# A causal convolution's filter sums moved wholly onto TensorE, with their tile moves in ScalarE's queue

## The reference, cut to what matters

```
def conformer_conv(h, w_pw1, b_pw1, w_dw, b_dw, ln_g, ln_b, w_pw2, b_pw2):
    u = h @ w_pw1 + b_pw1
    a, gate = jnp.split(u, 2, axis=-1)
    u = a * jax.nn.sigmoid(gate)
    u = lax.conv_general_dilated(
        u, w_dw[:, None, :], window_strides=(1,), padding=[(CONV_WIDTH - 1, 0)],
        dimension_numbers=("NWC", "WIO", "NWC"), feature_group_count=CONV_CHANNELS) + b_dw
    u = jax.nn.silu(layernorm(u, ln_g, ln_b))
    return u @ w_pw2 + b_pw2
```

## Time and profile before

| | us |
|---|---|
| median of 3 runs | 1313.1 (1306.43 to 1316.91) |
| the profiled execution | 1311.96 |
| its span in the trace | 1310.6 |
| TensorE busy | 1210.4 (92%) |
| VectorE busy | 960.3 (73%) |
| ScalarE busy | 653.4 (50%) |

### The profile page before, as it was taken

One profiled execution on the slowest core, in us unless ns is written; L12 is line 12 of the kernel. 1 busy time (PEld: TensorE's weight loads), 2 busy tenths in 40 slices (PEclk: granted clock), 3 DMA queues, 4 the chain that ended last, 5 costly groups with the idle time before them and its releaser, 6 DMA issues.

```text
span 1310.6 us, 24770 instructions
## 1 busy us (share of the span) xinstructions
PE 1210.4 (92%) x9796; PEld 1152.6 (88%) x9796; DVE 960.3 (73%) x1853; ACT 653.4 (50%) x1142; POOL 108.7 (8%) x106
## 2 busy tenths in 40 slices
PE   4978899999998999999978788999989879999999
PEld 4957899999987999999967678999989767999999
DVE  5966598878776888878886658888875555766653
ACT  5326554445446544445555664544444765545431
POOL 2001100002000200004000112000011112100000
PEclk9999899999999999999998989999999989999999
DMA  7487688877853678787633325887865422555552
GB/s 275 142 210 92 225 301 261 252 265 265 271 179 123 196 262 263 236 276 249 219 110 103 103 91 177 272 255 252 275 230 184 133 89 83 191 179 186 184 193 65
DMA packets 81126, 259.36 MB, mean 198 GB/s; under 512 B 8904, under 2 KB 20424, under 8 KB 81012
## 3 DMA queue, kind: packets, MB, share of 16 engines
q1 hardware_dynamic: 81012, 257.79, 62.1%
HBM read 252.68 MB, written 5.08 MB: 197 GB/s over the span
## 4 chain that ended last, share of the span: by engine, by line
PE 68%; DVE 18%; ACT 6%; issue 4%; DMA 1%; POOL 1%; DVEq 0%; ACTq 0%
PE ps L521 61%; DVE wlo L1188 6%; DVE aacc L1194 2%; DVE CV L1194 1%; PE ps L582 1%; DVE X L1194 1%; DMA raw<-wall 1%; ACT HH L840 1%; ACT oS L840 1%; PE ps L617 1%; ACT eS L840 1%; PE ps L613 1%; PE ps L612 1%; PE ps L621 1%; DVE tn L1191 1%
## 5 line engine op out<-in xcount | busy, mean ns | idle before, releaser
L521 PE MATMUL ps<-HH,whi 128*128 128x256 f32 (+1 forms) x2152 | 625.7, 291 | 32.9 <-DVE wlo L1188 13.9
L521 PE MATMUL ps<-HH,wlo 128*128 128x256 f32 (+1 forms) x2152 | 615.3, 286 | 0.0
L521 PE MATMUL ps<-HL,whi 128*128 128x256 f32 (+1 forms) x2152 | 615.0, 286 | 0.0
L840 ACT ACTIVATE whi<-raw 128x1024 fp32r<-128x1024 f32 x363 | 381.0, 1056 | 333.3 <-PE ps L521 328.0
L1188 DVE TENSOR_TENSOR wlo<-raw,whi 128x1024 fp32r<-128x1024 f32 x363 | 444.2, 1228 | 37.2 <-ACT whi L840 36.7
L521 PEld LDWEIGHTS ps<-HH,whi 128*128 128x128 f32 x2152 | 415.7, 193 | 51.7 <-issue 22.4
L521 PEld LDWEIGHTS ps<-HL,whi 128*128 128x128 f32 x2152 | 415.6, 193 | 0.4
L521 PEld LDWEIGHTS ps<-HH,wlo 128*128 128x128 f32 x2152 | 415.4, 193 | 0.0
L521 PE MATMUL ps<-GH,whi 128*128 128x256 f32 x704 | 198.2, 282 | 0.6 <-DVE bcol L1414 0.5
L521 PE MATMUL ps<-GL,whi 128*128 128x256 f32 x704 | 197.5, 281 | 0.0
L521 PE MATMUL ps<-GH,wlo 128*128 128x256 f32 x704 | 197.5, 280 | 0.0
(11 more groups left out here) (207 smaller groups left out, 984.7 us busy)
## 6 DMA issues: line engine op xcount, KB each, us to landing
raw<-wall SPq DMA_DIRECT2D x363, 512.0 KB, 4.3
araw<-ada SPq DMA_DIRECT2D x96, 512.0 KB, 4.7
UR<-uscr SPq DMA_DIRECT2D x24, 142.0 KB, 3.3
scratch<-bvec SPq DMA_DIRECT2D x1, 3072.0 KB
oBB<-kbias SPq DMA_DIRECT2D x16, 192.0 KB, 2.5
aTB<-scratch SPq DMA_DIRECT2D x12, 128.0 KB, 2.4
X<-x_in SPq DMA_DIRECT2D x2, 512.0 KB, 5.9
out<-X SPq DMA_DIRECT2D x8, 128.0 KB, 3.1
```

The source lines that it names most:

```text
L521: ins = pe.e.matmul(o, l, r, start=(kt == p.order[0] and i == 0), stop=(kt == p.order[-1] and i == 2))
L840: ac.then_inc(ac.e.activation(o, i, func, **kw), sem)
```

## The change

- All eight channel tiles go the way over PE. The 62 multiply-adds on DVE are gone; DVE builds eight sets of diagonals instead of six, in three buffers, each now behind the `U` tile and behind the use of the buffer (`cvt`).
- PE takes the filter sums of channel tile j (`taps(j)`) inside `pw1`, behind tile 2j+7 (`TAPS_AFTER = 6` tiles behind the start of its pair), for j = 0 to 4, and those of tiles 5, 6 and 7 behind `pw1`. The channel sum of tile j-1 follows `taps(j)` at once.
- `taps_out` and `taps_in` are issued by ACT, between its high parts and sigmoids, and ACT waits for the write to DRAM before it issues the reads.
- The bias rows have 384 numbers instead of 512, and `scratch<-bvec` is issued by SP at `pw1` tile 7, behind the load of unit 15.
- In the normalisation DVE makes each rest one step later.

```
+TAPS_AFTER = 6
+                def taps(j):
+
+                    bk = bank[5 + j % 2]
+                    pe.wait_ge(S.dg, j + 1)
+                    pe.wait_ge(S.ur[j % 3], 64 * (j // 3 + 1))
+                    if j >= 2:
+                        pe.wait_ge(S.cva, j - 1)
+                    for m in range(8):
+                        for r in range(4):
+                            ins = pe.e.matmul(bk[32 * r:32 * r + 32, 0:T], DG[j % 3][:, 8 * r + m, :],
+                                              UR[j % 3][:, r, 4 * m:4 * m + T], start=(m == 0), stop=(m == 7))
+                    pe.then_inc(ins, S.cvt)
+                    if j:
+                        channel_sum(j - 1)
+
+                def channel_sum(j):
+                    pe.wait_ge(S.bv, 1)
+                    pe.wait_ge(S.cva, j + 1)
+                    return pe.e.matmul(bank[7][:, 0:T], ones[:, :], CV[:, j, :], start=(j == 0), stop=(j == KD - 1))
...
+                    j, odd_tile = divmod(nt - TAPS_AFTER, 2)
+                    if odd_tile and j >= 0:
+                        taps(j)
...
+                for j in range((16 - TAPS_AFTER) // 2, KD):
+                    taps(j)
+
+                pe.then_inc(channel_sum(KD - 1), S.lnt)
...
+                def taps_out(j):
+                    ac.wait_ge(S.u, j + 1)
+                    ac.wait_ge(S.uz, 2)
+                    load(uscr[j], U[:, j, :], S.uw[j % 3])
+
+                def taps_in(j):
+
+                    if j >= 3:
+                        ac.wait_ge(S.cvt, j - 2)
+                    ac.wait_ge(S.uw[j % 3], 16 * (j // 3 + 1))
+                    for c in range(4):
...
+                def taps(j):
+                    ac.wait_ge(S.cvt, j + 1)
+                    act(CV[:, j, :], bank[5 + j % 2][:, 0:T], ACT.Identity, S.cva, bias=V("bdw", j))
...
+                    if nt % 2 == 0 and nt:
+                        taps_out(nt // 2 - 1)
+                    if nt % 2 and nt > 1:
+                        taps_in(nt // 2 - 1)
...
+                    if odd_tile and j >= 0:
+                        taps(j)
                 warm()
+                taps_out(KD - 1)
+                taps_in(KD - 1)
+                for j in range((16 - TAPS_AFTER) // 2, KD):
+                    taps(j)
...
-                    if nt >= 4:
-                        for _ in range(4):
-                            tap()
...
-            sp.wait_ge(S.bv, 1)
-            load(scratch, bvec[:, :].unsqueeze(1).broadcast_to([12, P, 512]), S.bd)
+            for nt in tiles("pw1"):
+                if nt == 7:
+                    sp.wait_ge(S.bv, 1)
+                    load(scratch, bvec[:, :].unsqueeze(1).broadcast_to([12, P, NB]), S.bd)
```

More of the change, by code:

```diff
@@ L20 @@
 UW = T + 28
+NB = P + T
 NEG = -1e30
@@ L48 @@
 ODD = (8, 0, 1, 2, 10, 3, 9, 4, 5, 6, 7, 11)
-CONV_DVE = (0, 1)
-CONV_PE = tuple(j for j in range(KD) if j not in CONV_DVE)
+TAPS_AFTER = 6
 class Product:
@@ L333, in __init__ @@
         self.ara = [new(f"ara{i}") for i in range(ARAW)]
-        self.uw = [new(f"uw{i}") for i in range(len(CONV_PE))]
+        self.uw = [new(f"uw{i}") for i in range(3)]
         self.ur = [new(f"ur{i}") for i in range(3)]
@@ L410, in program @@
             CV = sb("CV", [P, KD, T], F32, st)
-            DG = {j: sb(f"DG{j}", [P, 32, 32], F32, st) for j in CONV_PE}
+            DG = [sb(f"DG{i}", [P, 32, 32], F32, st) for i in range(3)]
             UR = [sb(f"UR{i}", [P, 4, UW], F32, st) for i in range(3)]
@@ L570, in after @@
                         pe.wait_ge(S.sd, 1)
-                        pe.then_inc(pe.e.matmul(bank[7][0:12, :], rels[:, :], ohs[:, :], start=True, stop=True), S.relm)
+                        pe.then_inc(pe.e.matmul(bank[7][0:12, 0:NB], rels[:, :], ohs[:, :], start=True, stop=True), S.relm)
                 product("pw1", HH[NORM_SET[0]], HL[NORM_SET[0]], T, norm_ready(0), after)
[L574 to L592, removed]
+                for j in range((16 - TAPS_AFTER) // 2, KD):
+                    taps(j)
+                pe.then_inc(channel_sum(KD - 1), S.lnt)
                 for kt in range(KD):
@@ L840, in act, with load @@
                 ac.then_inc(ac.e.activation(o, i, func, **kw), sem)
+            def load(o, i, sem):
+                ac.then_inc(ac.e.dma_start(o, i), sem, 16)
             def highs(upto):
@@ L938, in convolution @@
                         act(TMP[nt % 8][:, :], TMP[nt % 8][:, :], ACT.Sigmoid, S.sig, bias=V("bp1", 8 + nt // 2))
-                for n, j in enumerate(CONV_PE):
-                    ac.wait_ge(S.cvt, n + 1)
-                    act(CV[:, j, :], bank[5 + n % 2][:, 0:T], ACT.Identity, S.cva, bias=V("bdw", j))
+                    j, odd_tile = divmod(nt - TAPS_AFTER, 2)
+                    if odd_tile and j >= 0:
+                        taps(j)
                 warm()
+                taps_out(KD - 1)
+                taps_in(KD - 1)
+                for j in range((16 - TAPS_AFTER) // 2, KD):
+                    taps(j)
                 for kt in range(KD):
@@ L1307, in convolution @@
             def convolution():
[L1308 to L1318, removed]
                 dv.then_inc(dv.e.memset(epsb[:, :], EPS), S.eps)
@@ L1342, in convolution @@
                         dv.wait_ge(S.kmask, 16)
[L1343 to L1346 removed]
+                        tt(bvec[:, :], bank[7][0:12, 0:NB], msk[:, :], ALU.add, S.bv)
                     n, t = nt // 2, TMP[nt % 8]
@@ L1368, in convolution @@
                 inverse(1)
-                for kt in range(KD + 1):
+                for kt in range(KD + 2):
                     if kt < KD:
@@ L1839, in sync_program @@
             load(msk[:, :], kmask, S.kmask)
-            def taps_out(n):
-                sp.wait_ge(S.u, CONV_PE[n] + 1)
-                sp.wait_ge(S.uz, 2)
-                load(uscr[n], U[:, CONV_PE[n], :], S.uw[n])
-            def taps_in(n):
-                if n >= 3:
-                    sp.wait_ge(S.cvt, n - 2)
-                sp.wait_ge(S.uw[n], 16)
-                for c in range(4):
-                    src = bass.AP(uscr.tensor, uscr.offset + n * P * (31 + T) + c, [[31 + T, 32], [32 * (31 + T), 4], [1, UW]])
-                    load(UR[n % 3][32 * c:32 * c + 32, :, :], src, S.ur[n % 3])
-            for nt in range(17):
-                if nt < 16:
-                    lows(low_to("pw1", nt))
-                for n, j in enumerate(CONV_PE):
-                    if nt == 2 * j + 2:
-                        taps_out(n)
-                        if n < 3:
-                            taps_in(n)
-            for n in range(3, len(CONV_PE)):
-                taps_in(n)
-            sp.wait_ge(S.bv, 1)
-            load(scratch, bvec[:, :].unsqueeze(1).broadcast_to([12, P, 512]), S.bd)
+            for nt in tiles("pw1"):
+                if nt == 7:
+                    sp.wait_ge(S.bv, 1)
+                    load(scratch, bvec[:, :].unsqueeze(1).broadcast_to([12, P, NB]), S.bd)
             rest("pw2")
```

36 lines of the change are left out of this document (18 added, 18 removed).

## The result

The changed kernel takes 1326.23 us in the median (1325.09 to 1328.77, 4 runs) against 1312.85 for the kernel before (1306.43 to 1316.91, 4 runs beside it). The ratio is 1.0109, with a 95% interval of 1.0065 to 1.0153: about 1% slower. The forecast was 1316, no change that a measurement can tell; the range, 1304 to 1331, holds the time, and the value lies near the end that rival B gave. The profiled execution has a span of 1325.5 us, 14.9 more than before.

The account below looks back on a forecast made before the run. It took PE to bound pw1, with a weight unit queued behind the bias rows' write waiting until nearly all of it is through. 1312.0 + 9.4 at the channel sums' end - 5.0 at gu0 = 1316.4, said as 1316; range 1304 to 1331.

Parts of the forecast that it names:

- rival B: Longer stall: the write's time goes by its rows, tile moves' packets take turns with it; 1331 us, 1.5% slower; chance 0.18.
- What bounds, and PE alone: Up to the channel sums' end: pw1 bound by PE, not by DVE's multiply-adds; PE alone ends them at 101.2.
- N: End of the channel sums behind pw1: 101.8 us before, forecast 111.2, so +9.4 us.
- the stall: ACT waiting in pw1 for weight unit 16, from about 62.5 to 80.2; without it, channel sums end at 102.8.
- The time of the bias rows' write: SP's write issued at 44.9 in pw1: 29.9 us by bytes plus 5.4, so unit 16 usable at 80.2; by rows, 90.1.
- the tile moves on ACT pass the write: In pw1: SP and ACT own separate rings that DMA engines go round between, so only weights behind the write wait.
- PE stalls at a filter sum for its reads: Sign of being wrong: it would put the fault on the moves in ACT's queue and not on the weights.
- if the moves waited too: Channel tile 2's reads would come after 80, fifteen us late, and the channel sums end some 15 us later still.
- The issues on ACT: Per tile pair in pw1: five issues at 0.44 us each, 2.2 us; ACT's work, some 5.2 of 9.8 us, is covered.
- What comes back at `gu0`: Late weights cost 5.0 us at gu0's start, by comparison with gu1 and gu3; -5.0 taken, bounds 0 and 7.0.
- Rival A: Write through early or weights pass it, so ACT never stalls at unit 16; 1308 us, best end 1304; chance 0.22.
- Rival C: The 5.0 us at gu0 don't come back, ACT being late with units 21 to 24; 1321 us; with mixtures 0.15.

Follow-up runs that it names:

- one_row: Changed kernel with each bias row written once instead of 128 times, leaving the relative bias wrong: 1309.65 us, ratio 0.9992 to the kernel before.
- sp_moves: Changed kernel with the tile moves back in SP's queue and the bias rows' write behind the last of them: 1308.94 us, ratio 0.9986.
- late_write: Changed kernel with the bias rows' write back behind all of the first product's weight units, still 384 wide: 1334.61 us, ratio 1.0176.
- pool_moves: Changed kernel with tile moves issued and waited for by GpSimd instead of ScalarE, the early write kept: 1335.85 us, ratio 1.0194.
- pieces_early: Changed kernel with the early write cut in eight, one piece at each of pw1 tiles 7 to 14: 1315.78 us, ratio 1.0026.
- wide_early: Changed kernel, write at the same early place, but bias rows made on 96 partitions and each written 16 times: 1309.20 us, ratio 0.9986.
- before_one_row: Kernel before with each bias row written once instead of 128 times, leaving the relative bias wrong: 1318.31 us, ratio 1.0060.
- wide_after_moves: Changed kernel with the write made from 96 partitions and issued behind the last tile reads: 1309.03 us, ratio 0.9984.
- before_narrow: Kernel before with bias rows 384 wide instead of 512 and nothing else changed: 1310.78 us, ratio 1.0010.
- before_early: Kernel before with bias rows 384 wide and their write issued at tile 7 of the first product: 1340.22 us, ratio 1.0224.
- write_after_moves: Changed kernel with the twelve-partition write issued only when the last channel tile's reads have landed: 1309.58 us, ratio 0.9982.

## Why the prediction came out as it did

*What bounds, and PE alone.* Right. One channel tile's sums measured 3.66 us with 3.56 used, `pw1` in one_row ends where it should, and N without the stall is 102.7 for 102.8 forecast. That the exchange gains nothing at N is shown by sp_moves and one_row: without the 62 multiply-adds on DVE and with two more tiles on PE, N moves by 0 to 1 us. What each of the two is worth alone no run tells.

*The time of the bias rows' write.* Right, and to the microsecond. Unit 16 was to be usable at 80.2, and it landed at 45.35 + 34.6 = 80.0. So the time goes by bytes and not by rows, which would have given 90.1, and the weights do wait for the write. ACT had no use for the unit then: it was still behind.

*Where the prediction failed* is the sentence "By that the tile moves on ACT pass the write and only the weights wait". They don't pass it. The write of channel tile 3 took 15.3 us, the one in late_write 19.6, those in pool_moves 17.7 and 18.7. So PE's stall began at the bias of channel tile 0, at 59 us, and not at 77.9 with bias 2; unit 16, for which ACT was to wait from 62.5, had landed 4.7 us before ACT reached it at 84.75. From 80 to N are 41 us and not 31. The sum had the reads of channel tile 4 issued at 81.2; in fact the reads of tile 3 and the write of tile 4 were still to come, and those reads were issued at 87.69, 6.5 us later. From there to N are 33.1 us where the sum had 30.0. The two together are the 9.6 us at N (120.8 for 111.2). The prediction's own sign came true, that PE stalls at a filter sum for its reads: 4.6 us at channel tile 2. The price was in view: I had written that, if the moves waited too, N would lie some 15 us higher, and gave it no chance of its own.

*The rule I leaned on.* The Trainium skill ("DMA: Bandwidth & Descriptors", section "Queues, rings and completion order") does say that an engine goes round between rings; it also says that it drains a whole packet before it switches, 9 to 17 descriptors as a rule and 64 at most. An estimate by the Trainium skill's upper figure: SP's queue moved 644 rows of the twelve-partition write in 13 us (late_write, 92 to 105 us), 0.24 us for a row of each partition, and 64 of these, a row counted as a descriptor, are 15.5 us. No run here shows the length of a turn, so that figure stays the Trainium skill's.

The prediction had taken it that going round costs a small move nothing, and gave no length of a turn. The landings of 15 to 20 us beside the long write, from ACT's queue and from GpSimd's, are this case's own. pieces_early fits a wait of that kind: behind pieces of 16 rows, 3.9 us by the same rate, the moves land in at most 7.6 us.

*The issues on ACT.* Taken at 0.44 us each from SP's rows; three of them took 4.9 to 5.05. The trace of before had such an issue: in the same view as the earlier trace rows, SP's issues of weights have a maximum of 4.9 us. I quoted the landings of that view and not its issues:

```profile
L1782 SPq DMA_DIRECT2D raw<-wall x11: 327/332/4915, 118.3 to 148.1; - x11
```

*What comes back at `gu0`.* -5.0 was mis-sized; it is -1.8 to -3.1 in all twelve kernels (G - N). The comparison with `gu1` and `gu3` was the wrong one. Without the long write, in one_row, the 25 us before G still hold only 174 matmuls (windows, also of 142 to 147 us):

```profile
124.50:149.50 25.00, 22.23 (x174) 22.03 (x174) 18.03 (x28) 16.19 (x28) 9.38 (x9) 0.93 0.49 152
142.00:147.00 5.00, 5.00 (x33) 5.00 (x33) 3.63 (x4) 3.40 (x4) 0.00 (x0) 0.71 0.62 204
```

That is 17.5 fewer than the mean of the two other places, by the prediction's count 2.1 of the 5.0 us, and it belongs to this place and not to the late weights: PE is idle for 2.8 us, and the granted clock is 0.71 in the 5 us behind that, where before `gu1` they are 1.6 us idle and a clock of 1.00.

*The rest.* -2.9 us came back behind G, in stretches that the change doesn't touch; see the last point below. So 1316.4 became 1312.0 + 19.0 - 1.8 - 2.9 = 1326.3, half a microsecond under the profiled execution's 1326.8. Rival B had the right direction and size and the mechanism half right: the moves did land late beside the write, but the write's time did not go by its rows. Rival A was refuted. Rival C, that the 5.0 us don't come back, was right for 3.2 of them, but not by its cause, units that ACT makes late: one_row, where nothing waits for the write, gets back no more.

That 1326.23 lies within 1304 to 1331 is in good part luck. The forecast was no change that can be told, and the measured 1.1% can be told; the time is just past the 1326 above which the prediction gave a chance of 0.18. The upper end of the range came from rival B's longer write, which there was not, and 2.9 us came back for which the sum had no reason.

## What to carry to other kernels

A transfer that is out of the way in its own queue is not out of the way of the others: before one is moved earlier, list every transfer of every queue that will be in flight beside it, and take the landings of all of them from a place where both ran. And when work leaves a queue, ask what its order had guaranteed; here the bias write had been kept behind the tile moves only by standing in the same queue. A slow transfer is worth a look at its GB/s first: from eight times the partitions this one moved at 376 GB/s instead of 78, and then its place didn't matter.

## What the runs showed of the hardware

- Twelve partitions written 128 times each move at 79 GB/s with rows of 2 KB (before) and 78 with rows of 1.5 KB (late_write); 96 partitions written 16 times each, same bytes and row length as the latter, at 376 GB/s (wide_early; 2304 KB landed in 12.9 us).
- A 143.5 KB move issued beside the twelve-partition write lands in 15 to 20 us, issued by ScalarE (15.3, 19.6) or GpSimd (17.7, 18.7); the moves of one_row, without the write, land in 2.3 to 6.7.
- The issue of a move held ScalarE for up to 5 us (5053 ns) while that write ran (changed), and the issue of weight unit 16 held SP for 9.6; without the write (one_row) no move's issue took over 0.81 us. What the issue waits for no run shows.
- Reads of 128 KB by 128 partitions land in 8.1 us in the median from one DRAM row of 2 KB (before_one_row), in 4.1 from one of 1.5 KB (one_row), and in 2.4 from rows of their own (before).
- The stretch from `mixd` to `gu1`, the same program in all kernels but for the reads of the two one-row ones, took 104.7 or 104.8 us in eight of the profiled executions, 106.5 in before and 109.5 or 109.6 in wide_after_moves, before_narrow and before_early (115.0 in before_one_row, whose reads are slower), without a link to the edit that I could find; it is left open. It is as large as the repaired kernels' gain over the kernel before, of which the largest on record is 0.2% (write_after_moves, 0.9982, at most 0.3% by its interval).
